# Per-head core of the gated DeltaNet layer: keys and queries in a PSUM bank each, cross-block exponentials by an activation bias, one exponential set moved

## The chip, the cores and the metric

The kernel runs on one core of a Trainium2 chip. The metric is the time of the whole kernel on the device in microseconds (us), the median of its runs. A profile is one execution recorded by the hardware profiler. Its rows name the engines PE (TensorE; PEld are its weight loads), DVE (VectorE), ACT (ScalarE), POOL (GpSimd) and SP (SyncE, which issues most DMAs; SPq is its queue of issues).

## The reference

A two-layer encoder on 256 tokens of width 2048. Layer 0 is a bidirectional gated DeltaNet, layer 1 a Conformer convolution, and each is followed by a SwiGLU FFN. The part that matters here is the DeltaNet between its input and its output projection, for 16 query/key heads with two value heads each, in two directions (4 combinations c per head):

```
decay = exp(where(incl, g[..., :, None] - g[..., None, :], -inf))
lower = where(strict, einsum(k_beta, k) * decay, 0)
sol   = triangular_solve(eye + lower, [v * beta, k_beta * exp(g)])     # u, w
a_qk  = einsum(q, k) * decay
v_new = u_i - w_i @ S ;  o_i = q_g @ S + a_i @ v_new ;  S = S * cd + k_tail.T @ v_new
o     = rmsnorm(o_f + o_b, norm_w) * silu(z)
```

## The kernel before, in words

Most of the kernel streams weights through TensorE. Between the last tile of the z projection and the output projection stands the core stage, which this change is about: 16 heads, one after the other, in a software pipeline written out by hand. Every engine has its own function `step(s)` with a fixed order of blocks, and semaphores join them. In step s an engine works for head s (A), prepares head s+1 (M), and finishes heads s-1 (B), s-2 (C) and s-3 (E). The two halves of the sequence (tiles t of 128 tokens) are treated as one block system of 256, instead of chunks of 64 with a carried state.

For a head, the rows of cumulated log decays (`rr`, 1 MB, broadcast to all partitions), keys and queries (`qk`), values (`vt`), the gate (`zt`) and the inverses of the 32x32 diagonal blocks (`inv_a`, `inv_b`, or `nat_c` with `trn_c`) are loaded by SP in the order of `core_loads`. DVE adds row and column sums into `exb` (`decay_sums`), for three segments of 128 columns: two diagonal ones with a triangular mask (L1433) and one off the diagonal (L1431). ACT takes the exponential of all three in one instruction into `dec` (`decays`, L2011), four for the keys (kind 0) and four for the queries (kind 1). PE makes key-key and key-query products for both (L965), 512 columns each, into one buffer, `psg[:, 0]`, and DVE multiplies them into `dec` (`keys` and `queries`, L1475).

PE in step s runs in this order: W (L920, 32x32 products), the transposes of a finished head (L691), X (L939), TN and T (L951, L959), the key and query products KQ (L965), Y (L974), U1 (L908), N (L991), O (L1009, twelve products that make the head's output), and U0 (L908). ACT in step s copies the output (`os`, L2023), copies U0's result (`uu`, half 0, L2028), copies W's (`wtc`), squares the output (L2037), copies the transposes (`oT`), scales the values by beta (`rv`, L2051), takes the key exponentials D0, copies Y's result (`yb2`, L2060) and U1's (`uu`, half 1, L2063), copies N's into `turned` (L2068), and takes the query exponentials D1 of the next head, which wait until O has read the old ones. These letters are used below. X cannot start before `uu` half 0 is there, N waits for `yb2`, and O for `uu` half 1.

`uu` and `trn_c` lie in a free slot of the weight ring. One `rr` buffer serves all heads, so its load waits until DVE has read the old one. Two heads of three load their inverse blocks with 8 DMAs, every third (heads 2, 5, 8, 11, 14) with 16, since its two parts lie apart. After the last head the output projection runs on PE (`go_tile`, L701), its first tiles between the last steps.

Of the kernel before, what the change touches and what calls it, by code (L numbers as in the profile page):

```python
# [14 lines left out]
P = 128  # L15
# [49 lines left out]
def build(nc, x_in, c_in, ada_w, ada_b, norm_w, gdn_in_w, gdn_conv_w, gdn_A_log, gdn_dt_bias,  # L65
# [31 lines left out]
    with stack:  # L97
# [95 lines left out]
        nat_c = sb("nat_c", [P, 4, TT, P], at=p2a)  # L193
        tri0 = sb("tri0", [P, 2, P], at=p2a)
        sb("core_gap", [P, 2, P], at=p2a)
        exb = sb("exb", [P, 2, 4, 2, 3, P], at=p2a)
# [144 lines left out]
        qk_land, rr_land, v_land, z_land = (sem(n) for n in ("qk_land", "rr_land", "v_land", "z_land"))  # L341
        inv_land = [sem(f"inv_land{i}") for i in range(3)]
        kq_done = sem("kq_done")
# [89 lines left out]
        def _(sp):  # L433
# [79 lines left out]
            def load_rr(h, to=rr):  # L513
                sp.dma_start(to[:, :, :].rearrange('p c t -> p (c t)'), d_rr[ds(h, 1)].rearrange("a c t -> (a c t)").partition_broadcast(P)).then_inc(rr_land, 16)
# [60 lines left out]
            for z in range(NZ):  # L575
                for j in range(4):
                    load_w(G_Z + 4 * z + j, (G_Z + j) % 4, rows4(gdn_in, j * KT * P, QKV + z * NSL))
                if z == 5:
# [6 lines left out]
                    load_rr(0, rr0)  # L585
# [9 lines left out]
            sp.wait_ge(c_init, C_CONST + 4)  # L595
# [91 lines left out]
        def _(pe):  # L687
# [212 lines left out]
            def step(s):  # L900
# [92 lines left out]
                if B:  # L993
# [17 lines left out]
                    i.then_inc(o_done, 1)  # L1011
                if A:
# [135 lines left out]
        def _(dve):  # L1148
# [273 lines left out]
            def decay_sums(h):  # L1422
                dve.wait_ge(rr_land, 16 * (h + 1))
                if h > 1:
                    dve.wait_ge(d1_done, h - 1)
                for c in range(4):
                    for seg, t, kind, tj in ((0, 0, 0, 0), (2, 1, 0, 1), (1, 1 - c // 2, 1, c // 2)):
                        to, row = exb[:, h % 2, c, :, seg, :], (rr if h else rr0)[:, 2 * c:2 * c + 2, t * P:(t + 1) * P]
                        col = ncum[:, kind, tj, c, h:h + 1]
                        if seg == 1:  # L1430
                            i = ts(to, row, col, 0.0, ADD, MIN)  # L1431
                        else:
                            i = stt(to, row, col, tri0[:, c // 2:c // 2 + 1, :].broadcast_to([P, 2, P]), ADD, MIN)  # L1433
                i.then_inc(ex_done, 1)

            left = list(range(31))
            for n in range(4 * NZ):
# [21 lines left out]
                if n == 27:  # L1459
                    assert not left  # L1460
                    dve.wait_ge(c_init, C_CONST)
                    decay_sums(0)

            kqs = psg[:, 0, :, :].rearrange("p t (k n) -> p t k n", k=2)
# [18 lines left out]
            def queries(h):  # L1483
                dve.wait_ge(kq_done, h + 1)
# [3 lines left out]
            def step(s):  # L1488
# [887 lines left out]
```

## Time and profile before

| | us |
|---|---|
| median of 3 runs | 3102.44 (3100.78 to 3105.87) |
| the profiled execution | 3102.02 |
| its span | 3100.4 |
| PE busy | 2878.0 (93%) |
| DVE busy | 2188.0 (71%) |
| ACT busy | 1258.9 (41%) |

The span is cut into 40 slices of 77.5 us by the page; the core stage fills some three of them (from about 725 to 975 us). Shares of the whole span say little on it, so all rows below are from inside that stage, except those on the price of an ACT instruction.

### The profile page before, as it was taken

The page shows a single profiled execution, that of the slowest core. Times are in us where ns is not written, and L with a number is a line of the kernel's source. Part 1 is how long each engine was busy: PE and PEld are TensorE (multiplying, and loading weights), DVE is VectorE, ACT ScalarE, POOL GpSimd, SP SyncE. Part 2 cuts the span into 40 slices and gives each one's busy share as a digit, 9 for nine tenths or more (in the row PEclk, how much of TensorE's full clock was granted, in tenths as well). Part 3 has the DMA queues.
Part 4 walks back from the last instruction along what each step waited for, and adds up shares of the span by engine and source line. Part 5 has one row for each costly group of instructions (what it writes and reads, how often), then busy time and mean ns, then how long its engine had stood idle before and what let it go on. Part 6 is the DMA issues. An engine that isn't in the chain of part 4 may idle for free.

```text
span 3100.4 us, 38632 instructions
## 1 busy us (share of the span) xinstructions
PE 2878.0 (93%) x14244; PEld 2275.9 (73%) x14244; DVE 2188.0 (71%) x2273; ACT 1258.9 (41%) x1381; POOL 159.6 (5%) x304
## 2 busy tenths in 40 slices
PE   1699999997889989999999999899798999999998
PEld 1678888875665868888888887444686888888886
DVE  7599989876883758877778785189857555555555
ACT  2356644335673444333333333310345333333333
POOL 0011211122111000000000000000000000000000
PEclk8799999998999989999999999999899999999998
DMA  9777787665554967988888896344255655555663
GB/s 400 276 252 278 281 297 246 200 224 179 171 153 131 383 230 295 341 308 313 306 315 319 317 338 217 122 149 147 72 188 219 217 203 203 203 203 204 215 204 120
DMA packets 322817, 731.67 MB, mean 236 GB/s; under 512 B 48769, under 2 KB 64977, under 8 KB 294289
## 3 DMA queue, kind: packets, MB, share of 16 engines
q1 hardware_dynamic: 316896, 709.85, 64.6%
q0 software_dynamic: 5808, 20.35, 1.9%
q8 instruction: 66, 1.08, 0.1%
q14 instruction: 47, 0.38, 0.0%
HBM read 710.45 MB, written 19.69 MB: 235 GB/s over the span
## 4 chain that ended last, share of the span: by engine, by line
PE 83%; DVE 8%; DMA 3%; ACT 2%; issue 2%; SPq 2%; DVEq 0%; POOL 0%; ACTq 0%; POOLq 0%
PE psg L714 45%; PE psg L720 22%; PE psg L701 7%; DMA aring<-in_ada_w 2%; SPq L532 1%; PE psn L741 1%; PE pst L691 1%; DVE wlo L1156 1%; PE psg L965 1%; PE psn L1119 1%; DVE y L1671 1%; DVE cv L1380 1%; PE psn L1009 1%; DVE aacc L1255 1%; PE psn L691 1%
## 5 line engine op out<-in xcount | busy, mean ns | idle before, releaser
L1795 ACT ACTIVATE whi<-wraw 128x2048 fp32r<-128x2048 f32 x400 | 766.2, 1916 | 1221.6 <-PE psg L720 1112.7
L1156 DVE TENSOR_TENSOR wlo<-wraw,whi 128x2048 fp32r<-128x2048 f32 x400 | 917.7, 2295 | 476.8 <-ACT whi L1795 474.6
L714 PE MATMUL psg<-whi,h_hi 128*128 128x512 f32 x2304 | 731.5, 399 | 23.1 <-DVE h_lo L1751 13.2
L714 PE MATMUL psg<-whi,h_lo 128*128 128x512 f32 x2304 | 719.8, 394 | 0.0
L720 PE MATMUL psg<-wlo,h_hi 128*128 128x512 f32 x2304 | 572.3, 391 | 7.4 <-DVE wlo L1156 7.4
L714 PEld LDWEIGHTS psg<-whi,h_hi 128*128 128x128 f32 x2304 | 435.7, 191 | 115.9 <-issue 25.7
L714 PEld LDWEIGHTS psg<-whi,h_lo 128*128 128x128 f32 x2304 | 439.6, 191 | 93.9
L720 PEld LDWEIGHTS psg<-wlo,h_hi 128*128 128x128 f32 x2304 | 433.8, 188 | 98.8 <-DVE wlo L1156 8.9
L1166 DVE SCALAR_TENSOR_TENSOR aacc<-aring,cond,aacc 128x2048 f32<-128x2048 f32 x150 | 351.8, 2345 | 6.1 <-DMA aring<-in_ada_w 5.6
L701 PE MATMUL psg<-wraw,aring 128*128 128x512 f32 x512 | 221.1, 592 | 0.0
L714 PE MATMUL psg<-whi,g_hi 128*128 128x512 f32 x704 | 219.5, 393 | 0.0
L714 PE MATMUL psg<-whi,g_lo 128*128 128x512 f32 x704 | 219.0, 393 | 0.0
L701 PEld LDWEIGHTS psg<-wraw,aring 128*128 128x128 f32 x512 | 96.8, 190 | 118.5 <-issue 118.5
L720 PE MATMUL psg<-wlo,g_hi 128*128 128x512 f32 x704 | 173.9, 389 | 0.0
L714 PEld LDWEIGHTS psg<-whi,g_lo 128*128 128x128 f32 x704 | 133.7, 190 | 28.1
L714 PEld LDWEIGHTS psg<-whi,g_hi 128*128 128x128 f32 x704 | 133.8, 190 | 27.6
L720 PEld LDWEIGHTS psg<-wlo,g_hi 128*128 128x128 f32 x704 | 132.2, 188 | 27.4
L1590 DVE TENSOR_TENSOR y<-psg,y 128x1024 f32<-128x1024 f32 x88 | 107.5, 1222 | 61.7 <-PE psg L720 60.8
L1671 DVE SCALAR_TENSOR_TENSOR y<-glu,vec,y 128x242 f32 (+14 forms) x360 | 139.8, 465 | 0.0
L1380 DVE SCALAR_TENSOR_TENSOR cv<-pst,vec,cv 128x254 f32<-128x254 f32 (+1 forms) x256 | 117.2, 480 | 22.5 <-DVE cv L1378 0.3
L2329 POOL DMA_DIRECT2D d_cw<-cwc x4 | 4.7, 1176 | 2018.0 <-DVE cwc L1236 2017.2
L1475 DVE TENSOR_TENSOR dec<-dec,psg 128x512 f32<-128x512 f32 x120 | 58.3, 547 | 30.5 <-PE psg L965 15.8
(276 smaller groups left out, 2359.1 us busy)
## 6 DMA issues: line engine op xcount, KB each, us to landing
aring<-in_ada_w SPq DMA_DIRECT2D x192, 1024.0 KB, 7.0
wraw<-in_ffn_in_w SPq DMA_DIRECT2D x176, 1024.0 KB, 6.6
wraw<-in_gdn_in_w SPq DMA_DIRECT2D x96, 1024.0 KB, 5.2
wraw<-in_ffn_out_w SPq DMA_DIRECT2D x88, 1024.0 KB, 5.3
wraw<-in_cf_pw_w SPq DMA_DIRECT2D x48, 1024.0 KB, 5.2
wraw<-in_gdn_out_w SPq DMA_DIRECT2D x32, 1024.0 KB, 8.1
wraw<-d_rr SPq DMA_DIRECT2D x15, 1024.0 KB, 5.9
x<-in_x SPq DMA_DIRECT2D x2, 2048.0 KB, 8.4
```

The lines of the kernel that those rows point to most:

```text
L532: sp.dma_start(to[32 * q:32 * q + 32, :, t, 32 * q:32 * q + 32], inv_view[ds(h, 1), t, q, :, s0:s1].rearrange("a i s j -> (a i) s j")).the ...
L691: return nc.tensor.transpose(dst, src, ident[:, :])
L701: i = mm(ps[:, t, :], a[:, kc, t * P:(t + 1) * P], wraw[:, slot, j * NSL:(j + 1) * NSL], start=first and j == 0, stop=last and j == len(kc ...
L714: mm(ps[:, t, 0:width], a[:, kc, t * P:(t + 1) * P], wh, start=first and j + n == 0, stop=False)
L720: i = mm(ps[:, t, 0:width], a_hi[:, kc, t * P:(t + 1) * P], wl, start=False, stop=last and j == len(kcs) - 1)
L1156: tt(wlo[:, j % 2, :], wraw[:, j % 4, :], whi[:, j % 2, :].bitcast(F32), SUB).then_inc(w_lo, 1)
L1166: stt(acc, ring[:, par, :], c, acc, MUL, ADD).then_inc(a_used, 1)
L1380: i = stt(dst, src, w, dst, MUL, ADD)
L1475: i = tt(to, to, kq.unsqueeze(1).broadcast_to(list(to.shape)), MUL)
L1590: tt(yj, psg[:, (s0 + par) % 2], yj, ADD).then_inc(ps_read, 1)
L1671: i = stt(dst, src, w, dst, MUL, ADD)
L1795: av(whi[:, j % 2, :], wraw[:, j % 4, :], ACT.Copy).then_inc(w_hi, 1)
```

## The change

Storage. `uu` gets memory of its own, and the third set of inverse blocks (`inv_c`) becomes one piece in the ring slot, so every head loads its blocks with 8 DMAs. There are two `rr` buffers (`rr_even`, `rr_odd`), each with its semaphore, released when D1 of its head is done.

Exponentials. `exb` keeps only the two diagonal segments: DVE's four instructions at L1431 are gone for each head. ACT makes the off-diagonal segment straight from the row buffer, with the column sum as bias (a value per partition). A set of four ACT instructions of 384 columns becomes four of 256 and four of 128 with bias.

Products. The key products (2 x 256 columns) stay where KQ was, but wait for `la_done` instead of `aq_done`. The query products (2 x 256 columns, QQ) go to the other bank of `psg[:, 0]` and stand behind O and ahead of U0. SP loads the next keys and queries after QQ.

Order. On DVE the subtraction L1515 and the copies of TN and T go ahead of `queries`, between two halves of the sums. On ACT, D1 is taken in the head's own step, behind the copies of U0 and W and ahead of `os`; `os` thus comes behind `uu` half 0; and `yb2` is copied ahead of D0. The copies at L2051 (values) and L2068 stay on ACT.

```diff
-        nat_c = sb("nat_c", [P, 4, TT, P], at=p2a)
+        uu = sb("uu", [P, 2, 4, P], at=p2a)
...
-        exb = sb("exb", [P, 2, 4, 2, 3, P], at=p2a)
+        exb = sb("exb", [P, 2, 4, 2, 2, P], at=p2a)
+        rr_even = sb("rr_even", [P, 8, T], at=p2a)
...
-        free_slot = wraw[:, (G_GO + 3) % 4, :].rearrange("p (a b c m) -> p a b c m", a=2, b=4, c=TT)
-        trn_c = free_slot[:, 0]
-        uu = free_slot[:, 1].rearrange("p b c m -> p (b c m)").rearrange("p (o c m) -> p o c m", o=2, c=4)
-        rr = wraw[:, (G_GO + 1) % 4, :].rearrange("p (c t) -> p c t", t=T)
-        rr0 = exb[:, 1].rearrange("p c k s m -> p (c k s m)")[:, 1024:3072].rearrange("p (c t) -> p c t", t=T)
-        inv_a = wraw[:, (G_GO + 2) % 4, :].rearrange("p (s t m) -> p s t m", s=8, t=TT)
+        rr_odd = wraw[:, (G_GO + 1) % 4, :].rearrange("p (c t) -> p c t", t=T)
+        inv_a, inv_c = (wraw[:, (G_GO + n) % 4, :].rearrange("p (s t m) -> p s t m", s=8, t=TT) for n in (2, 3))
         inv_of = tuple(h % 3 for h in range(HQ - 1)) + (1,)
-        natural = tuple((inv_a[:, 0:4], inv_b[:, 0:4], nat_c)[n] for n in inv_of)
-        turned = tuple((inv_a[:, 4:8], inv_b[:, 4:8], trn_c)[n] for n in inv_of)
+        inverse = tuple((inv_a, inv_b, inv_c)[n] for n in inv_of)
+        natural = tuple(a[:, 0:4] for a in inverse)
+        turned = tuple(a[:, 4:8] for a in inverse)
         inv_last = tuple(max((g for g in range(h) if inv_of[g] == inv_of[h]), default=None) for h in range(HQ))
-        inv_at = tuple(16 * (16 if inv_of[h] == 2 else 8) * inv_of[:h + 1].count(inv_of[h]) for h in range(HQ))
+        inv_at = tuple(128 * inv_of[:h + 1].count(inv_of[h]) for h in range(HQ))
...
-                if inv_of[h] == 2:
-                    parts = ((natural[h], 0, 4), (turned[h], 4, 8))
-                else:
-                    parts = (((inv_a, inv_b)[inv_of[h]], 0, 8),)
-                for to, s0, s1 in parts:
-                    for t in range(TT):
-                        for q in range(4):
-                            sp.dma_start(to[32 * q:32 * q + 32, :, t, 32 * q:32 * q + 32],
-                                         inv_view[ds(h, 1), t, q, :, s0:s1].rearrange("a i s j -> (a i) s j")).then_inc(inv_land[inv_of[h]], 16)
+                for t in range(TT):
+                    for q in range(4):
+                        sp.dma_start(inverse[h][32 * q:32 * q + 32, :, t, 32 * q:32 * q + 32],
+                                     inv_view[ds(h, 1), t, q].rearrange("a i s j -> (a i) s j")).then_inc(inv_land[inv_of[h]], 16)
...
             def core_loads(s):
 
                 if s + 2 < HQ:
-                    sp.wait_ge(ex_done, s + 2)
+                    sp.wait_ge(d1_done, s + 1)
                     load_rr(s + 2)
-                if s + 2 == HQ:
-                    sp.wait_ge(ex_done, HQ)
-                    go_raw(1)
-                    sp.wait_ge(u1_done, 13)
-                    go_raw(2)
                 if s + 1 < HQ:
                     sp.wait_ge(rv_done, s + 1)
                     load_v(s + 1)
+                if s + 2 == HQ:
+                    sp.wait_ge(u1_done, 13)
+                    go_raw(2)
                 if s + 2 < HQ - 1:
                     if inv_last[s + 2] is not None:
                         sp.wait_ge(u1_done, inv_last[s + 2] + 1)
...
                 if s + 1 == HQ - 1:
                     sp.wait_ge(u1_done, inv_last[HQ - 1] + 1)
                     load_inv(HQ - 1)
+                if s + 1 == HQ:
+                    sp.wait_ge(d1_done, HQ)
+                    go_raw(1)
                 if s + 2 < HQ:
-                    sp.wait_ge(kq_done, s + 2)
+                    sp.wait_ge(qq_done, s + 1)
                     load_qk(s + 2)
                 if s == 1:
...
                     i.then_inc(t_done, 1)
                 if M:
                     pe.wait_ge(qk_land, 32 * (s + 2))
-                    pe.wait_ge(aq_done, s + 1)
+                    pe.wait_ge(la_done, s + 1)
                     for jt in range(2):
-                        i = mm(psg[:, 0, jt, :], qk[:, 0, jt * P:(jt + 1) * P],
-                               qk[:, :, :].rearrange("p k t -> p (k t)"), start=True, stop=True)
+                        i = mm(psg[:, 0, 0, jt * T:(jt + 1) * T], qk[:, 0, jt * P:(jt + 1) * P], qk[:, 0, :], start=True, stop=True)
                     i.then_inc(kq_done, 1)
                 if A:
...
                     i.then_inc(o_done, 1)
+                if M:
+                    pe.wait_ge(aq_done, s + 1)
+                    for jt in range(2):
+                        i = mm(psg[:, 0, 1, jt * T:(jt + 1) * T], qk[:, 0, jt * P:(jt + 1) * P], qk[:, 1, :], start=True, stop=True)
+                    i.then_inc(qq_done, 1)
                 if A:
...
-            def decay_sums(h):
-                dve.wait_ge(rr_land, 16 * (h + 1))
-                if h > 1:
-                    dve.wait_ge(d1_done, h - 1)
-                for c in range(4):
-                    for seg, t, kind, tj in ((0, 0, 0, 0), (2, 1, 0, 1), (1, 1 - c // 2, 1, c // 2)):
-                        to, row = exb[:, h % 2, c, :, seg, :], (rr if h else rr0)[:, 2 * c:2 * c + 2, t * P:(t + 1) * P]
-                        col = ncum[:, kind, tj, c, h:h + 1]
-                        if seg == 1:
-                            i = ts(to, row, col, 0.0, ADD, MIN)
-                        else:
-                            i = stt(to, row, col, tri0[:, c // 2:c // 2 + 1, :].broadcast_to([P, 2, P]), ADD, MIN)
-                i.then_inc(ex_done, 1)
+            def decay_sums(h, cs):
+                if cs[0] == 0:
+                    dve.wait_ge(rr_land[h % 2], 16 * (h // 2 + 1))
+                    if h > 1:
+                        dve.wait_ge(d1_done, h - 1)
+                for c in cs:
+                    for t in range(TT):
+                        i = stt(exb[:, h % 2, c, :, t, :], rows_of(h)[:, 2 * c:2 * c + 2, t * P:(t + 1) * P], ncum[:, 0, t, c, h:h + 1],
+                                tri0[:, c // 2:c // 2 + 1, :].broadcast_to([P, 2, P]), ADD, MIN)
+                if cs[-1] == 3:
+                    i.then_inc(ex_done, 1)
...
+            kqs = psg[:, 0, :, :].rearrange("p k (t n) -> p t k n", t=2)
...
             def queries(h):
-                dve.wait_ge(kq_done, h + 1)
+                dve.wait_ge(*((qq_done, h) if h else (kq_done, 1)))
                 dve.wait_ge(d1_done, h + 1)
                 decayed(h, 1, aq_done)
...
                 M, A, B, C = s + 1 < HQ, s < HQ, 0 <= b < HQ, 0 <= g < HQ
 
                 if M:
-                    decay_sums(s + 1)
+                    decay_sums(s + 1, (0, 1))
+                if B:
+                    dve.wait_ge(rv_done, b + 1)
+                    dve.wait_ge(x_done, b + 1)
+                    for d in range(2):
+                        r = rv[:, b % 2, 1, 2 * d:2 * d + 2, :]
+                        i = tt(r, r, ps_a[:, 2 * d:2 * d + 2, :], SUB)
+                    i.then_inc(r2_done, 1)
                 if A:
-                    if s:
-                        queries(s)
                     dve.wait_ge(tn_done, s + 1)
                     for d in range(2):
                         (lead, rest), slot = halves(d, 64 * d), slot_of(2 * d)
                         i = nc.vector.tensor_copy(natural[s][rest, slot:slot + 2, :, lead], ps_tn[rest])
                     i.then_inc(tn_ok, 1)
+                    dve.wait_ge(t_done, s + 1)
+                    for d, b0 in QUADS:
+                        (lead, rest), slot = halves(d, b0), slot_of(2 * d)
+                        i = nc.vector.tensor_copy(turned[s][lead, slot:slot + 2, :, rest], ps_t[lead])
+                    i.then_inc(t64_done, 1)
+                if M:
+                    decay_sums(s + 1, (2, 3))
+                if A and s:
+                    queries(s)
                 if C:
                     dve.wait_ge(osq_done, g + 1)
                     ts(oms[:, 1, :], oms[:, 0, :], 1.0 / P, RMS_EPS, MUL, ADD).then_inc(oms_done, 1)
...
             def decays(h, kind, done):
 
                 for c in range(4):
-                    i = av(dec[:, h % 2, c, kind].rearrange("p s m -> p (s m)"),
-                           exb[:, h % 2, c, kind].rearrange("p s m -> p (s m)"), ACT.Exp)
+                    n = c // 2
+                    av(dec[:, h % 2, c, kind, 0:3:2, :], exb[:, h % 2, c, kind], ACT.Exp)
+                    i = av(dec[:, h % 2, c, kind, 1, :], rows_of(h)[:, 2 * c + kind, (1 - n) * P:(2 - n) * P], ACT.Exp,
+                           bias=ncum[:, 1, n, c, h:h + 1])
                 i.then_inc(done, 1)
 
             def step(s):
                 par, b, g, e = s % 2, s - 1, s - 2, s - 3
                 M, A, B, C, E = s + 1 < HQ, s < HQ, 0 <= b < HQ, 0 <= g < HQ, 0 <= e < HQ
 
-                if C:
-                    act.wait_ge(o_done, g + 1)
-                    if g:
-                        act.wait_ge(og_done, g)
-                    av(os[:, :, :], ps_o, ACT.Copy, scale=float(P) ** -0.5).then_inc(oc_ok, 1)
                 if B:
                     act.wait_ge(u0_done, b + 1)
                     if b:
...
                 if A:
                     act.wait_ge(w_done, s + 1)
                     av(wtc, ps_w, ACT.Copy, scale=-1.0).then_inc(wt_done, 1)
+                if A and s:
+                    if s > 1:
+                        act.wait_ge(o_done, s - 1)
+                    decays(s, 1, d1_done)
+                if C:
+                    act.wait_ge(o_done, g + 1)
+                    if g:
+                        act.wait_ge(og_done, g)
+                    av(os[:, :, :], ps_o, ACT.Copy, scale=float(P) ** -0.5).then_inc(oc_ok, 1)
                 if C:
                     act.wait_ge(oc_ok, g + 1)
                     if g:
...
                                 c = 2 * d + v
                                 i = av(rv[:, par, o, c, :], vt[:, t, v, :], ACT.Copy, scale=beta[:, t, c, s:s + 1])
                     i.then_inc(rv_done, 1)
+                if A:
+                    act.wait_ge(y2_done, s + 1)
+                    av(yb2[:, :, :, :], ps_y, ACT.Copy, scale=-1.0).then_inc(y2_ok, 1)
                 if M:
                     act.wait_ge(ex_done, s + 2)
                     if s:
                         act.wait_ge(x_done, s)
                     decays(s + 1, 0, d0_done)
-                if A:
-                    act.wait_ge(y2_done, s + 1)
-                    av(yb2[:, :, :, :], ps_y, ACT.Copy, scale=-1.0).then_inc(y2_ok, 1)
                 if B:
                     act.wait_ge(u1_done, b + 1)
                     av(uu[:, 1, :, :], ps_a, ACT.Copy).then_inc(uc1_done, 1)
...
                         f, r, slot = first(d), second(d), slot_of(2 * d)
                         i = av(turned[s][f, slot:slot + 2, :, r], ps_n[f], ACT.Copy)
                     i.then_inc(t128_ok, 1)
-                if M:
-                    if s:
-                        act.wait_ge(o_done, s)
-                    decays(s + 1, 1, d1_done)
             act.wait_ge(ex_done, 1)
             decays(0, 0, d0_done)
```

ACT before, from the copy of U1's result in one step to the same copy in the next (`uu` is in `wraw` here; `dec` with 384 columns is D1 the first time and D0 the second):

```order
L2063 ACTIVATE wraw<-pst 128x512
L2068 ACTIVATE wraw<-pst 64x4x64 x2
L2011 ACTIVATE dec<-exb 128x384 x4
L2023 ACTIVATE os<-psn 128x512
L2028 ACTIVATE wraw<-pst 128x512
L2031 ACTIVATE wtc<-psg 128x4x32
L2037 ACTIVATE osq,oms<-os 128x128 x4
L2041 ACTIVATE oT<-psn 128x512
L2051 ACTIVATE rv<-vt,beta 128x128 x8
L2011 ACTIVATE dec<-exb 128x384 x4
L2060 ACTIVATE yb<-pst 128x256
L2063 ACTIVATE wraw<-pst 128x512
```

Behind O's wait stands D1 and then `os`, ahead of the copy L2028 that X waits for.

ACT after, the end of one step and the start of the next (L2072 is the copy of U1's result, L2077 that into `turned`, L2028 the copy of U0's, L2031 that of W's):

```order
L2015 ACTIVATE dec<-exb 128x2x128
L2016 ACTIVATE dec<-wraw,ncum 128x128
L2015 ACTIVATE dec<-exb 128x2x128
L2016 ACTIVATE dec<-wraw,ncum 128x128
L2072 ACTIVATE uu<-pst 128x512
L2077 ACTIVATE wraw<-pst 64x4x64 x2
L2028 ACTIVATE uu<-pst 128x512
L2031 ACTIVATE wtc<-psg 128x4x32
```

Nothing but L2077 stands between the copies of U1's and of U0's result now.

ACT after, further on in the same step, where D1 ends (its last pair of instructions) and D0 begins (its first pair):

```order
L2015 ACTIVATE dec<-exb 128x2x128
L2016 ACTIVATE dec<-wraw,ncum 128x128
L2040 ACTIVATE os<-psn 128x512
L2046 ACTIVATE osq,oms<-os 128x128 x4
L2050 ACTIVATE oT<-psn 128x512
L2060 ACTIVATE rv<-vt,beta 128x128 x8
L2064 ACTIVATE yb<-pst 128x256
L2015 ACTIVATE dec<-exb 128x2x128
L2016 ACTIVATE dec<-rr_even,ncum 128x128
```

D1 and `os` have moved between L2028 and the values, and `yb` ahead of D0.

PE before, from the key and query products to X of the next step:

```order
L965 MATMUL psg<-qk 128x512 x2
L974 MATMUL pst<-nat_c,dec 64x64 x8
L908 MATMUL pst<-rv,inv_b 128x128 x4
L991 MATMUL pst<-wraw,yb 64x64 x8
L1009 MATMUL psn<-wraw,dec 128x128 x12
L908 MATMUL pst<-rv,wraw 128x128 x4
L920 MATMUL psg<-wraw,dec 32x32 x16
L691 MATMUL psn<-ident,og 128x128 x4
L939 MATMUL pst<-wraw,dec 128x128 x4
```

PE after, the same stretch (L973 is Y, L990 is N, L1008 is O, L1014 the query products QQ):

```order
L965 MATMUL psg<-qk 128x256 x2
L973 MATMUL pst<-wraw,dec 64x64 x8
L908 MATMUL pst<-rv,inv_b 128x128 x4
L990 MATMUL pst<-wraw,yb 64x64 x8
L1008 MATMUL psn<-uu,dec 128x128 x12
L1014 MATMUL psg<-qk 128x256 x2
L908 MATMUL pst<-rv,wraw 128x128 x4
L920 MATMUL psg<-wraw,dec 32x32 x16
L691 MATMUL psn<-ident,og 128x128 x4
L939 MATMUL pst<-uu,dec 128x128 x4
```

Half of the products left the place behind T and stand now between O and U0.

## Rows read from the trace of the kernel before

**Rows 1.** Windows: span, each engine's busy time (instructions), clock, DMA; core stage, one step.

```profile
737.25:949.95 212.70, 171.17 (x2478) 134.03 (x2479) 170.10 (x488) 148.69 (x462) 33.11 (x168) 0.93 0.52 156
855.60:868.30 12.70, 10.87 (x168) 8.70 (x168) 11.93 (x36) 10.22 (x33) 2.37 (x12) 1.00 0.49 151
```

**Rows 2.** Line L2028: count, ns shortest/median/longest, first and last start.

```profile
L2028 ACT ACTIVATE wraw<-pst x16: 592/592/597, 737.2 to 950.0; 128x512 f32<-128x512 f32 x16
```

**Rows 3.** Timeline of ACT, one step: start, us, instruction, [idle before, releaser].

```profile
854.45 0.60 ACT L2023 ACTIVATE os<-psn 128x512 f32<-128x512 f32 x1
854.95 0.59 ACT L2028 ACTIVATE wraw<-pst 128x512 f32<-128x512 f32 x1
...
855.58 0.32 ACT L2037 ACTIVATE osq<-os 128x128 f32<-128x128 f32 x1
...
857.23 2.44 ACT L2051 ACTIVATE rv<-vt,beta 128x128 f32<-128x128 f32 x8
859.56 1.76 ACT L2011 ACTIVATE dec<-exb 128x384 f32<-128x384 f32 x4
861.21 0.38 ACT L2060 ACTIVATE yb<-pst 128x256 f32<-128x256 f32 x1
861.76 0.60 ACT L2063 ACTIVATE wraw<-pst 128x512 f32<-128x512 f32 x1 [0.18 <-PE pst L908]
...
865.40 1.76 ACT L2011 ACTIVATE dec<-exb 128x384 f32<-128x384 f32 x4 [2.24 <-PE psn L1009]
...
867.68 0.59 ACT L2028 ACTIVATE wraw<-pst 128x512 f32<-128x512 f32 x1
```

**Rows 4.** Timeline of PE in the same step.

```profile
855.59 1.16 PE L939 MATMUL pst<-wraw,dec 128*128 128x128 f32 x8 [1.10 <-ACT wraw L2028]
...
858.07 1.95 PE L965 MATMUL psg<-qk 128*128 128x512 f32 x4 [0.68 <-DVE dec L1475]
859.96 0.68 PE L974 MATMUL pst<-wraw,dec 64*64 64x64 f32 x16
...
862.41 2.94 PE L1009 MATMUL psn<-wraw,dec 128*128 128x128 f32 x24
865.20 1.06 PE L908 MATMUL pst<-rv,wraw 128*128 128x128 f32 x8
866.18 0.45 PE L920 MATMUL psg<-inv_b,dec 32*32 32x32 f32 x32
```

**Rows 5.** Groups of ACT's instructions by line, with and without a per-partition operand.

```profile
L2051 ACT ACTIVATE rv<-vt,beta 128x128 f32<-128x128 f32 x128 | 39.1, 400 | 0.6 <-DMA vt<-d_v 0.6
...
L1980 ACT ACTIVATE bt<-bt,epsr 128x256 f32<-128x256 f32 x1 | 0.5, 509 | 0.0
L1978 ACT ACTIVATE bt<-bt 128x256 f32<-128x256 f32 x1 | 0.4, 419 | 0.0
```

**Rows 6.** Waits in the core stage: total us, times, longest.

```profile
PE psg L965 <- DMA qk<-d_qkn: 17.1, 5, 5.3
```

**Rows 7.** Timeline of PE behind idle gaps of four lengths.

```profile
803.22 1.96 PE L965 MATMUL psg<-qk 128*128 128x512 f32 x4 [1.45 <-DVE dec L1475]
...
788.01 3.67 PE L965 MATMUL psg<-qk 128*128 128x512 f32 x4 [3.58 <-DMA qk<-d_qkn]
...
830.04 3.78 PE L965 MATMUL psg<-qk 128*128 128x512 f32 x4 [2.20 <-DMA qk<-d_qkn]
833.75 1.12 PE L974 MATMUL pst<-inv_b,dec 64*64 64x64 f32 x16
834.80 1.62 PE L908 MATMUL pst<-rv,wraw 128*128 128x128 f32 x8
...
873.03 3.49 PE L965 MATMUL psg<-qk 128*128 128x512 f32 x4 [2.91 <-DMA qk<-d_qkn]
```

**Rows 8.** Windows behind the gaps of 1.45 and 2.20 us.

```profile
803.20:805.20 2.00, 1.98 (x6) 0.76 (x8) 1.88 (x8) 2.00 (x7) 0.77 (x4) 1.00 0.86 346
...
830.03:832.00 1.97, 1.96 (x3) 0.93 (x4) 1.21 (x5) 1.75 (x5) 1.39 (x8) 0.50 1.04 399
```

More of the change, by code:

```diff
@@ L206, in build, with rows_of @@
         oms = sb("oms", [P, 4, 4], at=p2a)
-        free_slot = wraw[:, (G_GO + 3) % 4, :].rearrange("p (a b c m) -> p a b c m", a=2, b=4, c=TT)
-        trn_c = free_slot[:, 0]
-        uu = free_slot[:, 1].rearrange("p b c m -> p (b c m)").rearrange("p (o c m) -> p o c m", o=2, c=4)
-        rr = wraw[:, (G_GO + 1) % 4, :].rearrange("p (c t) -> p c t", t=T)
-        rr0 = exb[:, 1].rearrange("p c k s m -> p (c k s m)")[:, 1024:3072].rearrange("p (c t) -> p c t", t=T)
-        inv_a = wraw[:, (G_GO + 2) % 4, :].rearrange("p (s t m) -> p s t m", s=8, t=TT)
+        rr_odd = wraw[:, (G_GO + 1) % 4, :].rearrange("p (c t) -> p c t", t=T)
+        inv_a, inv_c = (wraw[:, (G_GO + n) % 4, :].rearrange("p (s t m) -> p s t m", s=8, t=TT) for n in (2, 3))
         inv_of = tuple(h % 3 for h in range(HQ - 1)) + (1,)
-        natural = tuple((inv_a[:, 0:4], inv_b[:, 0:4], nat_c)[n] for n in inv_of)
-        turned = tuple((inv_a[:, 4:8], inv_b[:, 4:8], trn_c)[n] for n in inv_of)
+        inverse = tuple((inv_a, inv_b, inv_c)[n] for n in inv_of)
+        natural = tuple(a[:, 0:4] for a in inverse)
+        turned = tuple(a[:, 4:8] for a in inverse)
         inv_last = tuple(max((g for g in range(h) if inv_of[g] == inv_of[h]), default=None) for h in range(HQ))
-        inv_at = tuple(16 * (16 if inv_of[h] == 2 else 8) * inv_of[:h + 1].count(inv_of[h]) for h in range(HQ))
+        inv_at = tuple(128 * inv_of[:h + 1].count(inv_of[h]) for h in range(HQ))
+        def rows_of(h):
+            return rr_odd if h % 2 else rr_even
         oT = sb("oT", [P, HV, T], at=p2a)
@@ L339, in build @@
         inv_out0, inv_out = sem("inv_out0"), sem("inv_out")
-        qk_land, rr_land, v_land, z_land = (sem(n) for n in ("qk_land", "rr_land", "v_land", "z_land"))
+        qk_land, v_land, z_land = (sem(n) for n in ("qk_land", "v_land", "z_land"))
+        rr_land = [sem(f"rr_land{i}") for i in range(2)]
         inv_land = [sem(f"inv_land{i}") for i in range(3)]
-        kq_done = sem("kq_done")
+        kq_done, qq_done = sem("kq_done"), sem("qq_done")
         ex_done = sem("ex_done")
@@ L511, in load_qk, with load_rr @@
                 sp.dma_start(qk[:, 1, :], d_qkn[ds(h, 1)].rearrange("a p t -> p (a t)")).then_inc(qk_land, 16)
-            def load_rr(h, to=rr):
-                sp.dma_start(to[:, :, :].rearrange('p c t -> p (c t)'), d_rr[ds(h, 1)].rearrange("a c t -> (a c t)").partition_broadcast(P)).then_inc(rr_land, 16)
+            def load_rr(h):
+                sp.dma_start(rows_of(h)[:, :, :].rearrange('p c t -> p (c t)'), d_rr[ds(h, 1)].rearrange("a c t -> (a c t)").partition_broadcast(P)
+                             ).then_inc(rr_land[h % 2], 16)
             def load_v(h):
@@ L584, in _ @@
                     sp.wait_ge(rr_out, 16 * 8)
-                    load_rr(0, rr0)
+                    load_rr(0)
             store_inv()
@@ L594, in _ @@
             load_rr(1)
-            sp.wait_ge(c_init, C_CONST + 4)
+            sp.wait_ge(c_init, C_CONST + 3)
             load_inv(1)
@@ L1461, in _ @@
                     dve.wait_ge(c_init, C_CONST)
-                    decay_sums(0)
-            kqs = psg[:, 0, :, :].rearrange("p t (k n) -> p t k n", k=2)
+                    decay_sums(0, range(4))
+            kqs = psg[:, 0, :, :].rearrange("p k (t n) -> p t k n", t=2)
             kq0 = pst[:, :, :].rearrange("p (t k) n -> p t k n", t=2)
@@ L1509, in step @@
                        ).then_inc(oms_done, 1)
-                if B:
-                    dve.wait_ge(rv_done, b + 1)
-                    dve.wait_ge(x_done, b + 1)
-                    for d in range(2):
-                        r = rv[:, b % 2, 1, 2 * d:2 * d + 2, :]
-                        i = tt(r, r, ps_a[:, 2 * d:2 * d + 2, :], SUB)
-                    i.then_inc(r2_done, 1)
-                if A:
-                    dve.wait_ge(t_done, s + 1)
-                    for d, b0 in QUADS:
-                        (lead, rest), slot = halves(d, b0), slot_of(2 * d)
-                        i = nc.vector.tensor_copy(turned[s][lead, slot:slot + 2, :, rest], ps_t[lead])
-                    i.then_inc(t64_done, 1)
                 if M:
@@ L2057, in step @@
                     decays(s + 1, 0, d0_done)
-                if A:
-                    act.wait_ge(y2_done, s + 1)
-                    av(yb2[:, :, :, :], ps_y, ACT.Copy, scale=-1.0).then_inc(y2_ok, 1)
                 if B:
@@ L2318, in _ @@
             store_z(7, 1)
-            pr.inc(ms(nat_c[:, :, :, :], 0.0))
             pool.wait_ge(w_lo, G_GO)
-            pr.inc(ms(trn_c[:, :, :, :], 0.0))
+            pr.inc(ms(inv_c[:, :, :, :], 0.0))
             pool.wait_ge(inv_out0, 48)
```

## The prediction

> **What bounds the kernel now.** I read the page first for where the change lies. It touches only the core stage, so I took the window from the first to the last copy of U0's result, L2028. These are 16 instructions, the first at 737.25 and the last at 949.95 us, so 15 steps [rows 2]. In these 212.7 us no engine is full: PE 171.2, DVE 170.1, ACT 148.7 us busy [rows 1], which is 14.18 us a step. A stretch in which everyone is at 70 to 80% is bound by a ring of waits, so I next read the timelines of one step engine by engine.
>
> In the step shown ACT goes from one L2028 at 854.95 to the next at 867.68 us, 12.73 us, and waits in it 2.24 us ahead of L2011 for PE's O (L1009) [rows 3]. PE starts O at 862.41, just after ACT's copy L2063 (start 861.76), and waits 1.10 us for ACT's L2028 ahead of X (L939) [rows 4]. So the ring is: ACT from L2028 to L2063; PE's O; ACT's D1 and `os`; L2028 again. U0 on PE (865.20 to 866.26) lies beside D1 and costs nothing [rows 3, 4]. DVE is a close second, with 11.93 of 12.70 us busy [rows 1]; it is not full in the ring's steps.
>
> 12.7 us is the usual step and 14.18 the mean. Most of the rest comes from five steps in which PE waited for `qk`, 17.1 us in all [rows 6]. Every third head has 16 DMAs for its inverse blocks ahead of its keys and queries in SP's order.
>
> **The change part by part.** I follow the new order with the old durations. The profiled execution took 3102.02 us, 0.4 below the median of 3102.44, so the sum is made against 3102.
>
> *Exponentials.* Four instructions of 384 columns take 1.65 us of ACT (859.56 to 861.21) [rows 3]. The new set has four of 256 and four of 128 columns with a bias. The trace has an instruction of 256 columns without and with a value per partition: 419 and 509 ns. One of 128 with such a value takes 400 ns [rows 5], and eight of them take 2.44 us, thus 0.291 from start to start, 0.109 less than one lasts [rows 3]. So a pair occupies (0.419 - 0.105) + 0.291 = 0.605 us and a set 2.42, which is 0.77 more than now. Bounds: if the bias cost nothing, the pair would be 0.09 cheaper (0.36 for a set); if the start-to-start overlap of two kinds of instruction were lost, a pair would be 0.82 and a set 3.3. I take 2.42, since both halves have a near row.
>
> The Trainium skill (ScalarE: Activation LUTs, What ACT_TABLE_LOAD costs) prices a pointer operand at about 93 ns each; the 90 ns between the two rows of 256 columns agree [rows 5]. With the page's own figures a pair would be some 0.60 us, an estimate that leaves the sum as it is.
>
> *ACT between the copies of U0's and U1's results.* Now 861.76 - 854.95 = 6.81 us, of which 0.18 is a wait: 6.63 [rows 3]. The new order puts D1 (2.42) and `os` (854.95 - 854.45 = 0.50) into this stretch, and D0 grows by 0.77. That makes 10.32 us, all of it back to back: DVE's sums are ready for D0 long before ACT gets there at about 7.9.
>
> *PE between the copies of U1's and U0's results.* From the start of L2063 to O 0.65 us; O to U0's start 2.79; then the query products QQ, half of what stands at L965 (859.96 - 858.07 = 1.89, so 0.95); U0 0.98 to the next start plus 0.13 until ACT goes on [rows 3, 4]. In sum 5.50 us, in which ACT has only its copy L2063 itself and the short L2068 to do, some 1.3 us. D1 lay in this gap; now nothing does, and QQ has been put into it.
>
> *The new ring.* 10.32 + 5.50 = 15.82 us a step at full clock, against 12.73. Nothing else closes a longer one: ACT's own work is 10.32 + 1.3, about 11.6, and DVE loses four L1431 a head, so both are below it.
>
> *What goes.* The halved DMA count and the second `rr` buffer remove the waits for `qk` [rows 6]. Keys and queries are now asked for behind QQ, some 1.1 us ahead of L2028, and two issues and a landing fit ahead of KQ or cost nothing: PE has 2.8 us of idle time behind U1. DVE's four sums, the halved KQ and the early subtraction are off the ring too. So what they give is only that all steps become alike.
>
> *Sum at full clock.* Step 1 has no `os`, squares and `oT`: 15.82 - 0.50 - 1.65 (855.58 to 857.23) = 13.67 [rows 3]; step 2 lacks `oT` (a copy of 512 columns like `os`, 0.50): 15.32; step 15 has no D0 and no QQ: 15.82 - 2.42 - 0.95 = 12.45; twelve full ones make 189.84. Together 231.3, against 212.7: +18.6 us. The stages ahead and behind are not changed; the tail is PE's own `go_tile` work in both. I cost them at nothing, give or take 2.
>
> *TensorE's clock.* PE idles more in the new ring. From L2028 to the end of U1 there are 0.64 to X, 1.80 from X to KQ without its wait (858.07 - 0.68 - 855.59), 0.95, 0.68 for Y and 1.16 for U1, four products like X: about 5.2 [rows 4]; N has to wait for `yb`, which is done at 10.32 - 2.42 - 0.26 + 0.38 = 8.0. That is a gap of about 2.8 us. After N's 0.6, O waits for L2072 until 10.97: another 2.3. In the trace a gap of 1.45 us left the product L965 at 1.96 us and the clock at 1.00 (2.4 GHz); gaps of 2.20, 2.91 and 3.58 were followed by 3.78, 3.49 and 3.67 us for the same work, with a clock of 0.50 (1.2 GHz) behind the first [rows 7, 8]. That is 1.5 to 1.8 us lost, and behind the gap of 2.20 another 0.44 and 0.46 in Y and U1 (1.12 for 0.68, 1.62 for 1.16), together 2.7. In the new order what follows the gaps is O, QQ and U0, which are in the ring, so the loss is paid. Bounds: 0 a step if the clock holds, 2.7 if it falls as behind the gap of 2.20. I take 1.7, as the three rows of L965 have it, in 14 steps: +24 us.
>
> Sum: 3102 + 18.6 + 24 = 3145 us.
>
> **The rivals.**
> *The clock holds.* Then only the ring counts: 3102 + 19 = 3121 us. For it: the two gaps have N between them, and a gap of 1.45 us kept 2.4 GHz. Against it: the gap of 2.20 was enough [rows 7, 8]. The Trainium skill (TensorE: Matmul & The Clock Gate, What's actually happening) has the clock fall only after idle time of its own measure, and each of the two gaps by itself stays short of it; by that rule this rival is the outcome. The row behind the gap of 2.20 us, at 1.2 GHz, speaks against it, so it gets the smaller share.
> *The DMA waits were the price, and the new ring stays open* (the other side). If D1 ahead of `os` found ACT idle, as D1 does now, the step would stay at 12.7 and only the five waits would go: 15 x 12.7 = 190.5, so -22 us and 3080. It decides at ACT's wait ahead of L2028: under 2.6 us there, and the step is below 14.2 and the kernel not slower. I compute 4.2 (5.50 - 1.3). For it speaks only that DVE and ACT both look fuller than the ring in [rows 1]; against it PE's fixed order O, QQ, U0.
> *Keys and queries late.* If their landing takes over 4 us more than I reckon, KQ eats PE's idle time and then Y, `yb`, N and O slip. With 2 us a step beyond the forecast: 3175. Now a wait for it was up to 5.3 us [rows 6], but behind 16 issues that are gone.
> *The change trades evenly*: exponentials at the cheap bound in both sets (-0.72 us a step) and no fall of the clock: ring 15.1, 3111 us; to be within the measurement another 3 us would have to be missing.
>
> **How the numbers follow.** Forecast (ring 15.8 and a lower clock) 0.56; the clock holds 0.25; late keys 0.07; even 0.06; faster 0.06. The predicted time is the forecast's, 3145. Its own range is 3128 to 3160 (0.5 to 2.7 us lost per step, with ±2 elsewhere). The range to hold 8 in 10 takes in the rival of the clock at its lower bound and the highest loss: 3112 to 3162. A measurement of this kernel can tell about 0.2%, 6 us, from no change. Faster by more than that 0.06, within it 0.06, slower 0.88.
>
> **What would show it.** ACT idle about 4.2 us ahead of L2028 with U0 (L908) as releaser, in place of 2.24 ahead of the exponentials; L2016 at 400 ns; 15 steps of one length, 15.8 us or 1.5 to 2.7 more; the wait for `qk` gone; PE waiting for `yb` ahead of N; O at 2.9 us or longer with a clock of 1.00 or 0.5 in its window. I am wrong if ACT starts L2028 without a wait or if steps are under 14.2 us.

## Result, and the profile after

The changed kernel takes 3144.37 us in the median (3143.65 to 3144.60), the kernel before beside it 3101.61. The ratio is 1.0135, 95% interval 1.0117 to 1.0152: slower by 1.35%, 43 us. The forecast was 3145.

The stretch from the first to the last copy of U0's result, by the same two views as in [rows 1, 2]; the second window is one usual step:

```profile
L2028 ACT ACTIVATE uu<-pst x16: 597/597/599, 737.2 to 992.4; 128x512 f32<-128x512 f32 x16
```

```profile
737.20:992.40 255.20, 187.85 (x2566) 169.22 (x2567) 156.56 (x430) 167.94 (x582) 33.37 (x168) 0.81 0.43 129
874.70:891.80 17.10, 12.50 (x183) 11.25 (x187) 10.92 (x30) 11.51 (x40) 2.38 (x12) 0.80 0.42 125
```

255.2 against 212.7 us: the 42.5 us more are the whole result. The steps are alike now (16.6 to 17.6 us, the usual one 17.1; the last one, without D0 and QQ, 15.3). In a usual one DVE is busy 10.9 us and no longer close, ACT 11.5 us, and the granted clock of the stretch has fallen from 0.93 to 0.81.

ACT's timeline over the handover, which answers to [rows 3]:

```profile
874.73 0.60 ACT L2028 ACTIVATE uu<-pst 128x512 f32<-128x512 f32 x1 [5.54 <-PE pst L908]
...
882.38 0.37 ACT L2064 ACTIVATE yb<-pst 128x256 f32<-128x256 f32 x1
882.65 0.41 ACT L2015 ACTIVATE dec<-exb 128x256 f32<-128x256 f32 x1
882.95 0.39 ACT L2016 ACTIVATE dec<-rr_even,ncum 128x128 f32<-128x128 f32 x1
883.25 0.41 ACT L2015 ACTIVATE dec<-exb 128x256 f32<-128x256 f32 x1
...
885.04 0.58 ACT L2072 ACTIVATE uu<-pst 128x512 f32<-128x512 f32 x1
885.52 0.76 ACT L2077 ACTIVATE wraw<-pst 64x256 f32<-64x256 f32 x2
891.81 0.60 ACT L2028 ACTIVATE uu<-pst 128x512 f32<-128x512 f32 x1 [5.53 <-PE pst L908]
```

A pair of exponentials occupies 0.60 us (882.65 to 883.25). Behind L2077 ACT waits 5.53 us for PE's U0, where before it waited 2.24 us for O and then had D1 to do. PE in the same step, answering to [rows 4]:

```profile
878.80 1.16 PE L908 MATMUL pst<-rv,wraw 128*128 128x128 f32 x8
882.80 1.12 PE L990 MATMUL pst<-wraw,yb 64*64 64x64 f32 x16 [2.85 <-ACT yb L2064]
885.67 4.34 PE L1008 MATMUL psn<-uu,dec 128*128 128x128 f32 x24 [1.75 <-ACT uu L2072]
889.85 1.03 PE L1014 MATMUL psg<-qk 128*128 128x256 f32 x4
890.72 1.05 PE L908 MATMUL pst<-rv,wraw 128*128 128x128 f32 x8
```

```profile
882.80:883.95 1.15, 1.12 (x16) 0.93 (x16) 0.38 (x3) 1.15 (x5) 0.49 (x3) 0.50 0.30 58
885.67:889.85 4.18, 4.18 (x24) 4.18 (x25) 4.15 (x12) 0.60 (x2) 0.66 (x4) 0.65 0.24 37
889.85:896.10 6.25, 6.07 (x126) 5.14 (x124) 1.90 (x7) 4.26 (x16) 0.00 (x0) 1.00 0.35 101
```

N starts after an idle gap of 2.85 us at a clock of 0.50, which is 1.2 GHz. O takes 4.34 us where it took 2.94, with 0.65 on average over its window, so it begins at 1.2 and ends at 2.4 GHz; from QQ on the clock is 1.00.

The waits between 730 and 1000 us, in total us, times and longest:

```profile
ACT uu L2028 <- PE pst L908: 86.9, 16, 6.5
DVE rv L1501 <- PE pst L939: 62.0, 15, 5.5
...
PE pst L990 <- ACT yb L2064: 39.3, 15, 2.9
...
PE psn L1008 <- ACT uu L2072: 26.8, 14, 2.7
...
PEld psg L965 <- DMA qk<-d_qkn: 0.4, 1, 0.4
```

The wait for `qk` of [rows 6] is gone. It has given way to a wait of ACT that comes in every step.

### The profile page after: what moved, and what is told of

Same layout as the page of the kernel before. It is cut to its first block, busy times and chain, and to the rows that moved or that the text cites. A ratio compares the mean times of both kernels' runs of the same rounds, so it can differ in the third digit from the quotient of the medians.

```text
span 3143.0 us, 38775 instructions
## 1 busy us (share of the span) xinstructions
PE 2895.3 (92%) x14304; PEld 2311.1 (74%) x14304; DVE 2173.1 (69%) x2209; ACT 1279.5 (41%) x1509; POOL 160.4 (5%) x303
## 4 chain that ended last, share of the span: by engine, by line
PE 82%; DVE 8%; ACT 6%; DMA 2%; issue 2%; DVEq 0%; SPq 0%; ACTq 0%
PE psg L714 44%; PE psg L720 22%; PE psg L701 7%; PE psn L1008 2%; DMA aring<-in_ada_w 2%; DVE wlo L1160 2%; PE psn L741 1%; ACT dec L2015 1%; PE pst L691 1%; ACT dec L2016 1%; ACT rv L2060 1%; DVE cv L1384 1%; PE psn L1123 1%; DVE y L1674 1%; DVE aacc L1259 1%
## 5 line engine op out<-in xcount | busy, mean ns | idle before, releaser
L714 PE MATMUL psg<-whi,h_hi 128*128 128x512 f32 x2304 | 731.6, 399 | 23.1 <-DVE h_lo L1754 13.1
L1008 PE MATMUL psn<-uu,dec 128*128 128x128 f32 x384 | 70.7, 365 | 26.8 <-ACT uu L2072 26.8
```

The lines of the kernel that those rows point to most:

```text
L714: mm(ps[:, t, 0:width], a[:, kc, t * P:(t + 1) * P], wh, start=first and j + n == 0, stop=False)
L1008: i = mm(ps_o[:, 2 * t + v, :], dec[:, q, c, 1, seg, :], uu[:, o, c, :], start=n == 0, stop=n == len(terms) - 1)
```

## The experiments

Ten variants were timed, each against the kernel before on its chip. Ratios are to that kernel, with their 95% interval, and are taken from means; times in us are medians, and the two can differ by 2 to 4 us (the kernel before has medians of 3102.4 to 3103.2). A step is the distance between two copies of U0's result, read from ACT's timeline. "The stretch" is, as above, from the first to the last of these copies.

**The clock alone: TensorE kept busy in its gaps.** The products' results are not read.

```diff
+                if A and s:
+                    for _ in range(5):          # ahead of N's wait; 4 more ahead of O's
+                        mm(psg[:, 1, 0, P:3 * P], ident[:, :], vec[:, 0:2 * P], start=True, stop=True)
```

> The changed kernel with nine extra products of 256 columns per step on TensorE, whose results nobody reads: five ahead of N's wait, four ahead of O's wait. They only keep the engine busy in its two idle gaps. Theory (the fallen clock costs 1.5 to 1.8 us a step in O): O goes from 4.4 back to 2.94 us, the steps from 17.1 to 15.8, the time from 3144 to 3121 (3117 to 3125). Rival (O is slow for another reason, such as its operand uu in new memory): O stays at 4.4 us and the time at 3144 or above.

Measured: 3121.8 us, ratio 1.0062 (1.0048 to 1.0075). In its timelines of PE and of ACT:

```profile
885.31 0.68 PE L993 MATMUL pst<-inv_b,yb 64*64 64x64 f32 x16 [0.43 <-ACT yb L2070]
885.92 1.99 PE L997 MATMUL psg<-vec,ident 128*128 128x256 f32 x8
888.18 2.94 PE L1014 MATMUL psn<-uu,dec 128*128 128x128 f32 x24 [0.27 <-ACT uu L2078]
```

```profile
861.55 0.60 ACT L2034 ACTIVATE uu<-pst 128x512 f32<-128x512 f32 x1 [4.13 <-PE pst L908]
877.24 0.60 ACT L2034 ACTIVATE uu<-pst 128x512 f32<-128x512 f32 x1 [4.13 <-PE pst L908]
```

O is back at 2.94 us, the usual step lasts 15.69 us, ACT waits 4.13 us, and the stretch has a clock of 1.00 and lasts 232.6 us (255.2 in the changed kernel, 212.7 before). More work on TensorE made the kernel 22 us faster: the idle gaps cost the clock, and the clock cost at least those 22 us. The other 19 to 20 are the ring at full clock; by the interval of the ratio, 15 to 23. Some 2 of them are an effect of the extra products themselves, by an estimate from this trace: in the last step O starts at 966.29 us, where the four products ahead of it began at 964.46 and nothing else held it.

**QQ's place.** Once with U0 ahead of it, once between N and O.

```diff
 # e2: U0 comes ahead of QQ   # e5: this block stands ahead of O, U0 stays where it was
+                    u_stage(s, 0, u0_done)
                 if M:
                     pe.wait_ge(aq_done, s + 1)   # QQ, as in the change
```

> The changed kernel with U0 ahead of the query products QQ on TensorE, so QQ is no longer between O and the copy of U0's result. Theory (QQ stands in the ring): 0.95 us less in each of 14 steps, 3144 to 3131. Rival (the ring is bound elsewhere, so QQ is hidden): 3144.

> The changed kernel with the query products QQ between N and O, in TensorE's idle time ahead of O, where nothing that ScalarE waits for stands behind them but O itself. Theory (QQ was in the ring, and putting it behind U0 left it there, because it then stood ahead of W, whose copy ScalarE needs next): 0.9 to 1.0 us less a step, 3144 to 3131; to 3110 if the shorter idle time also keeps the clock up. Rival (QQ costs the ring nothing wherever it stands): 3144.

Measured: behind U0 3145.1 us (1.0136; 1.0120 to 1.0151), between N and O 3117.1 us (1.0052; 1.0039 to 1.0065). The first expectation failed. ACT's timeline of that run says why:

```profile
892.53 0.60 ACT L2028 ACTIVATE uu<-pst 128x512 f32<-128x512 f32 x1 [4.73 <-PE pst L908]
893.82 0.28 ACT L2031 ACTIVATE wtc<-psg 128x128 f32<-128x128 f32 x1 [0.69 <-PE psg L920]
```

The wait for U0 is 0.8 us shorter, and 0.69 us of it come back one instruction later, at the copy of W's result, since QQ now stands ahead of W; the usual step is 17.1 us as before. The ring goes through both copies. Between N and O QQ is out of it: the time lies between the two that the second expectation gave (3131 and 3110), and behind the first two the steps last 14.8 to 16.2 us. That is more of a gain than the 0.95 us of QQ, because it also fills part of the idle time (PE's wait ahead of O falls from 26.8 to 4.2 us in all, and O takes the short 2.94 us in some steps and 4.3 in others).

**Both together.** QQ between N and O, five extra products ahead of N and two ahead of QQ.

> The changed kernel with QQ between N and O and with seven extra products of 256 columns, whose results nobody reads, in TensorE's idle time (five ahead of N, two ahead of QQ). Theory (the clock's loss and QQ in the ring are two separate terms): ring of 15.8 - 0.95 = 14.85 us at full clock, 14 steps, 3121 - 13 = 3108. Rival (QQ in the gap gained only by the clock): 3121.

Measured: 3110.85 us (1.0028; 1.0017 to 1.0039), and steps of 14.82 us, 14.85 reckoned. So QQ is 0.87 us of the ring (15.69 - 14.82), some 12 us in 14 steps, and the rest of the 27 us that its move gained was clock.

**D1 back behind O.**

```diff
-                if A and s:
-                    if s > 1:
-                        act.wait_ge(o_done, s - 1)
-                    decays(s, 1, d1_done)
...
                     i.then_inc(t128_ok, 1)
+                if M:
+                    if s:
+                        act.wait_ge(o_done, s)
+                    decays(s + 1, 1, d1_done)
```

> The changed kernel with the query exponentials D1 back at the end of ScalarE's step, behind its wait for O, as before. Theory (D1 has to fill ScalarE's idle time): the part from U0's to U1's copy falls from 10.3 to 7.9 us, the rest is 0.65 + 2.94 + 2.42 = 6.0 us, so steps of 14.0: 3097 if the clock holds, 3118 if O still takes 4.4 us. Rival (the heavier exponentials and QQ cost it, not where D1 stands): 3140 or more.

Measured: 3130.7 us (1.0093; 1.0080 to 1.0107). The direction is the theory's, the size is half (14 us less than the changed kernel, where 26 were forecast with a slow O). Rows of ACT and of PE show two reasons:

```profile
892.17 0.42 ACT L2015 ACTIVATE dec<-exb 128x256 f32<-128x256 f32 x1 [0.95 <-DVE exb L1433]
...
899.82 0.42 ACT L2015 ACTIVATE dec<-exb 128x256 f32<-128x256 f32 x1 [4.01 <-PE psn L1008]
```

```profile
798.81 2.94 PE L1008 MATMUL psn<-uu,dec 128*128 128x128 f32 x24 [2.90 <-ACT uu L2068]
...
846.34 5.46 PE L1008 MATMUL psn<-uu,dec 128*128 128x128 f32 x24 [2.90 <-ACT uu L2068]
```

Without D1 ACT reaches D0 so early that it now waits for DVE's sums, which the new order on DVE puts behind the subtraction and the copies: 0.95 us here, mostly 0.6. And PE waits 2.9 us or more ahead of O in nearly every step. In two of the steps with D1 the clock was still up in O (1.00 at 798.81), and these two last 14.79 us; in the others O took 4.2 to 5.5 us (a clock of 0.51 at 846.34), D1 waited up to 4.9 us for it, and steps went up to 17.3. The gap that D1 had filled before the change was one at 2.4 GHz. At full clock the place of D1 is thus worth 0.9 us a step (15.69 - 14.79), by an estimate 1.5 without the wait for DVE's sums, and not its whole 2.4.

**The exponentials and the DMAs in the old order.** First the kernel before with 8 DMAs for every head, then the same with two row buffers and the biased exponentials.

```diff
-        nat_c = sb("nat_c", [P, 4, TT, P], at=p2a)
+        uu = sb("uu", [P, 2, 4, P], at=p2a)
...
+        inverse = tuple((inv_a, inv_b, inv_c)[n] for n in inv_of)
```

> The kernel before with the third set of inverse blocks in one piece and uu in memory of its own, so that every head has 8 DMAs for them; orders, products and exponentials as before. Theory (five waits for keys and queries and the low clock behind them make 14.2 out of 12.7 us a step): the waits go, 15 steps of 12.7, 3102 to 3080. Rival (another wait takes their place): 3095 or more.

> The kernel before with the storage of the change (8 DMAs a head, two row buffers) and its exponentials with a bias; orders and products as before. To be compared with the kernel before with 8 DMAs alone, 3084. Theory (both sets are in the old ring at 0.77 us more each): steps of 14.2, 3084 + 22 = 3106. Rival (VectorE, 11.9 of 12.7 us busy, is the bound, and its relief pays for the exponentials): 3084 or less.

Measured: 3084.1 us (0.9950; 0.9936 to 0.9963) and 3101.7 us (0.9997; 0.9988 to 1.0006). The first has the lowest median of this study. Its stretch lasts 198.4 us:

```profile
735.10:933.50 198.40, 166.18 (x2478) 130.76 (x2479) 170.11 (x488) 148.76 (x462) 33.10 (x168) 0.96 0.56 167
```

That is 14.3 us less than the 212.7 before; the medians differ by 18.3 and the ratio stands for 15.5, so the DMAs were worth 14 to 18 us. The 22 of the expectation stood for fifteen steps of 12.7. Ten of them are 12.6 to 12.7; the first lasts 17.8, the last 10.5, and in the other three KQ (L958 here) ran slowly. Two steps of this run, of 14.4 and 12.7 us, differ in little else:

```profile
823.37 3.52 PE L958 MATMUL psg<-qk 128*128 128x512 f32 x4 [0.69 <-DVE dec L1468]
...
850.31 1.96 PE L958 MATMUL psg<-qk 128*128 128x512 f32 x4 [0.68 <-DVE dec L1468]
```

The exponentials, with the second row buffer, then cost 17.6 us by the medians and 15.0 in the stretch (213.4), most steps lasting 14.05 to 14.4: DVE's relief (155.6 us busy in the stretch instead of 170.1) did not pay for them.

**The values in ACT's wait.** In the kernel before with 8 DMAs; then with `os` behind the two copies as well; last in the changed kernel with QQ between N and O. `values(h)` is the loop at L2051, which leaves its old place; the first head's values are scaled ahead of the first step.

```diff
                     i.then_inc(t128_ok, 1)
+                if M:
+                    values(s + 1)
```

> The kernel before with 8 DMAs a head and with the scaling of the next head's values moved into ScalarE's wait for O, behind the copy into turned and ahead of D1. Theory (what stands on ScalarE between the copies of U0's and U1's results is in the ring, and what stands in its wait for O is not): 2.34 us leave the ring, VectorE with 11.9 us a step becomes the bound, steps of 12.1, 3084 to 3076. Rival (VectorE already is the bound): 3084.

> As the run with the values in the gap, and os behind the copies of U0's and W's results. Theory: with VectorE as the bound another 0.5 us out of the ring gives nothing or 1 to 3 us, 3073 to 3076. Rival (the ring over TensorE and ScalarE is still the bound): 0.5 us a step, 7 us less than the other run.

> The changed kernel with QQ between N and O and with the scaling of the next head's values at the end of ScalarE's step, in its wait for O, QQ and U0. Here that wait is long enough (4.5 us against 0.5 + 0.7 + 2.3) and TensorE's own way from X to U1 (5.2 us) is shorter than ScalarE's (8.0 without the values), unlike in the kernel before. Theory (the ring is ScalarE's leg plus O and U0): 10.3 - 2.3 + 4.55 = 12.5 us a step: 3080 with a full clock, 3100 if O stays at 4.3 us. Rival (the values do not leave the ring, as in the kernel before): 3115.

Measured: 3095.4 us (0.9975; 0.9965 to 0.9986), 3087.8 us (0.9950; 0.9937 to 0.9962) and 3099.6 us (0.9986; 0.9977 to 0.9995). The first is 11 us slower than without the move (8 by the ratios), where 8 us less were expected. ACT's timeline and its waits in the stretch:

```profile
794.86 2.44 ACT L2017 ACTIVATE rv<-vt,beta 128x128 f32<-128x128 f32 x8 [6.55 <-DMA vt<-d_v]
...
825.45 0.59 ACT L2033 ACTIVATE uu<-pst 128x512 f32<-128x512 f32 x1
...
837.57 0.59 ACT L2033 ACTIVATE uu<-pst 128x512 f32<-128x512 f32 x1
...
870.18 0.38 ACT L2054 ACTIVATE yb<-pst 128x256 f32<-128x256 f32 x1 [2.51 <-PE pst L967]
871.26 0.60 ACT L2057 ACTIVATE uu<-pst 128x512 f32<-128x512 f32 x1 [0.69 <-PE pst L901]
```

```profile
ACT rv L2017 <- DMA vt<-d_v: 12.1, 5, 6.6
```

Three things happen. Where the values are there in time, the step lasts 12.1 us (825.45 to 837.57), as the theory had it and 0.5 less than without the move. Only 0.5 of the 2.34 us are gained, since ACT then waits for PE ahead of `yb` and of U1's result (0.97 and 0.69 us in such a step; the 2.51 us at 870.18 are behind a slow KQ): PE's own way from X to U1 was nearly as long as ACT's, as the wait of 0.18 us at L2063 in [rows 3] says. But ACT asks for the values some 7 us earlier in the step than before, and five times their load had not landed (it takes 6.5 us in the median from issue to landing, 3.3 without the move). One wait of 6.55 us makes a step of 18.7; the others, and the slow KQ in the step behind some of them, make steps of 12.9 to 14.1. The stretch is 6.0 us longer in all (204.4). The rest of the loss stands ahead of it: from ACT's last instruction before the core stage to the first copy of U0's result it is 23.1 us, and 17.8 without the move.

With `os` behind the copies as well, the shortest steps are 11.64 us, 0.5 less, as that expectation's rival had it, and the waits for values grow to 17.8 us in seven; the two profiled executions are equal (3093, the slowest of this variant), so the difference of the medians, 3095 to 3088, is not accounted for.

In the changed kernel with its halved KQ PE's way is shorter, and there the same move pays: 3117 to 3100, a stretch of 206.0 instead of 227.6 us, with steps of 13.15 us at best. The expected 12.5 was missed on ACT's side, in its timeline:

```profile
783.65 0.60 ACT L2040 ACTIVATE uu<-pst 128x512 f32<-128x512 f32 x1 [0.74 <-PE pst L908]
...
789.91 0.42 ACT L2015 ACTIVATE dec<-exb 128x256 f32<-128x256 f32 x1 [0.58 <-DVE exb L1433]
...
792.32 0.57 ACT L2073 ACTIVATE uu<-pst 128x512 f32<-128x512 f32 x1
```

From copy to copy ACT takes 8.67 us where 8.0 were reckoned, since it waits for DVE's sums ahead of D0, and O starts 0.63 us behind the second copy, as in the other runs. Most of the longer steps, up to 15.5 us, are those with QQ or O at a low clock, behind QQ's wait for DVE's `queries` (25.3 us in 14 waits), or with a wait for the values (up to 3.10 us). That the time meets the 3100 of the expectation is chance: it had been reckoned for an O of 4.3 us in every step, and O takes 2.94 in most.

## Why the prediction was right

*The ring.* Predicted 15.82 us at full clock; with the clock held it measured 15.69. Its ACT leg was 10.32 against 885.04 - 874.73 = 10.31, and ACT's wait 4.2 against 4.13. The pair of exponentials was 0.605 against 0.60. The sum at full clock, +18.6 us, stands against +19.4 measured (3121.8 - 3102.4), with an interval of 15 to 23. The usual steps were 0.13 us cheaper than reckoned; the first and the last were dearer (14.8 and 14.4 us against 13.67 and 12.45), the last in part by the extra products.

*The clock.* 1.7 us a step were taken from the products behind three gaps; 17.10 - 15.69 = 1.41 is the usual step's loss, and 2.3 and 1.9 in steps 2 and 3. In all 24 were reckoned and 22 to 23 measured. So the usual step is 1.3 us above 15.8, a little less than the 1.5 to 2.7 that were named. The rival that the clock holds had for it that each gap is short by itself. It fell: N began at 1.2 GHz behind 2.85 us in most steps, and O was slow in every step of the stretch. But the price was read off the length of single gaps, and that length does not decide either: behind a wait of 2.90 us O took 2.94 us or 5.46, and behind 0.69 us KQ could be slow. That the mean of three rows fitted is partly luck.

*The DMAs.* Right that their waits go and leave nothing. What they had cost is now measured in the old order, 14 to 18 us; the rival reckoned with 22.

*QQ.* "In the ring" was right, 0.87 for 0.95 us. What the text did not see is that the ring has a second way in, W and its copy, so the obvious repair would not have worked.

*The range.* The forecast's own 3128 to 3160 has its low end without the 2 us that it allows elsewhere; with them it is 3126 (3102 + 18.6 + 14 x 0.5 - 2).

*The rival that the ring stays open* fell at its own test: ACT's wait was to be under 2.6 us and is 5.5. None of the terms of the sum had the wrong sign. The ring at full clock came out 0.8 us dearer than reckoned and the clock some 2 us cheaper; the intervals do not settle so little, and that the total lies within 1 us is partly luck. Not tested alone: the second row buffer, the new order on DVE, and `yb` ahead of D0.

## What to carry to other kernels

Before moving a block from one place of an in-order engine to another, ask what that engine waits for in the place that it leaves. Behind O's wait D1 stood beside U0, and the ring held only the longer of the two; moved, it left QQ and U0 alone in that place, and both it and they are in the ring. The price is what now stands one after the other (0.9 to 1.5 us a step at full clock), and not the length of the block. Then follow the ring along both engines: the freed leg may be covered by the other engine's, or a second wait may stand right behind the first. Ask too what the moved block reads: the values were needed some 7 us earlier, and their load was then late. Waits on TensorE can be paid twice, by their length and by the clock behind them. And take a change apart: its storage part alone was worth 14 to 18 us, which the orders and the exponentials hid.

## What the runs showed of the hardware

An idle gap of 2.85 us, N's 1.1 us of 64x64 products and another gap of 1.75 us left TensorE at 1.2 GHz into O, in every usual step, and the same kernel with extra products in these gaps held 2.4 GHz (stretch clock 0.81 and 1.00). In some steps of the changed kernel, such as this one, the clock was still up when N began (1.00) and down in the O behind it (0.65 over its window):

```profile
899.88 0.68 PE L990 MATMUL pst<-inv_b,yb 64*64 64x64 f32 x16 [2.60 <-ACT yb L2064]
902.76 4.33 PE L1008 MATMUL psn<-uu,dec 128*128 128x128 f32 x24 [2.19 <-ACT uu L2072]
```

The length of the last gap does not tell which level follows. With D1 back behind O, a wait of 2.90 us was followed by O at a clock of 1.00 in one step and 0.51 in another. In the old order with 8 DMAs, KQ ran at 0.53 behind an idle 0.69 us and at 1.00 behind 0.68, with the same work and the same wait of 1.10 us ahead of X before it. What decides between such steps these runs do not show.
